# Conditioning units spread over other phases, one bank of their sums per chunk, and a phase's first splits issued ahead of its border

## The chip, the cores and the metric

The kernel runs on one core of one Trainium2 chip. The metric is the device time of one execution in microseconds (us). The kernel before takes 1564.28 us, the median of 3 runs (1564.01 to 1564.74). In the profile TensorE is PE (PEld is its weight load), VectorE is DVE, ScalarE is ACT, GpSimd is POOL, and SyncE (SP) issues the transfers of the weights.

## The reference, cut to what matters

256 tokens of width 1024 go through two blocks, all in float32. The first block has a gating mixer and an MLP, then an attention mixer and an MLP. The second block is conditioned by a vector `c`:

```python
cond = jax.nn.silu(c)
for i in range(2):
    mod = (cond @ ada_w[i] + ada_b[i]).reshape(B, 3, 3, 1024)   # ada_w[i]: 1024 x 9216
    shift, scale, gate = mod[:, :, 0], mod[:, :, 1], mod[:, :, 2]
    h = modulate(rms_norm(x, norm_g[i, 0]), shift[:, 0], scale[:, 0])
    x = x + 0.5 * gate[:, 0] * swiglu(h, ffn_w_in[i, 0], ffn_w_out[i, 0])   # 1024 -> 2 x 2816 -> 1024
    h = modulate(rms_norm(x, norm_g[i, 1]), shift[:, 1], scale[:, 1])
    x = x + gate[:, 1] * (pool_mixer(h) if i == 0 else conv_mixer(h))
    h = modulate(rms_norm(x, norm_g[i, 2]), shift[:, 2], scale[:, 2])
    x = x + 0.5 * gate[:, 2] * swiglu(h, ffn_w_in[i, 1], ffn_w_out[i, 1])
return rms_norm(x, final_g)
```

Each layer `i` of the second block has three sublayers, so there are six: ffn0, pool, ffn1, ffn2, conv_in/conv_out, ffn3. Each needs a shift, a scale and a gate of 1024 numbers out of `cond @ ada_w`.

## The kernel before, in words

**Phases and slabs.** The program is a fixed list of phases: gate_in, positions, gate_out, mlp0, qkv, attn, attn_out, mlp1, ffn0, pool, ffn1, ffn2, conv_in, conv_out, ffn3. All weights arrive in slabs of 128 x 2048 floats (1 MB, two transfers of 512 KB each) in a ring of 5 buffers. A float32 product is made of three matmuls: the weight is split into `w_hi` (a rounded copy) and `w_lo` (the rest), and so are the activations. ACT writes `w_hi` of a slab (`split_hi`, L527) and DVE writes `w_lo` (`split_lo`, L868), as soon as ACT is done. Both are called by `ahead(g)`, which splits slab g + 3 while PE works near slab g. A slab's buffer is loaded anew once PE has used the slab five earlier.

**Chunks.** An mlp phase has 8 chunks of 4 slabs and an ffn phase has 11 chunks of 3 slabs. In a chunk PE does the up product of chunk c (48 matmuls for two token tiles, t = 0 and 1), then the down product of chunk c - 1, and then it transposes `mid`, the activated result of chunk c (L1422), into one of the two banks of `tr_ps`. In an ffn, ACT takes the silu of the up product (`pre`, L769), DVE multiplies (`mid`, L1181), and after the transpose ACT writes `hT_hi` (L537) and DVE `hT_lo` (L878). In the last chunk of an ffn PE runs: up product, transpose of tile 0, part of the down products, transpose of tile 1, and the rest of the down products in halves of 512 columns, each of which signals `acc_ready`.

**Borders.** Between two phases stands `enter`. DVE adds the two halves of tile 0 to the residual (L977 and L980), ACT squares and sums them (L547), POOL makes the inverse root in two small steps (`msq`, L499, and `rstd`, L493), DVE scales the rows (`xn`, L884), and PE transposes them (L1422). Then tile 1 follows in the same way, while PE begins the next phase with tile 0. The lists `before` and `after` of `enter` name slabs that are split inside the border: `before` between the residual of tile 0 and its scaling on DVE, and ahead of the squares on ACT, `after` behind the border.

**Conditioning.** `cond @ ada_w` isn't done on PE. Its 9216 columns per layer are 18 units of 512 columns, 36 in all. A unit is loaded in two halves of 1 MB by ACT's queue (`load_ada`, L596), and DVE multiplies each half into `ada_acc` in four steps (`ada`, L938 and L941), which leaves partial sums over 128 partitions. `load_ada` makes ACT wait until DVE has used the buffer that is loaded over. `ADA_AT` says which units a phase does. Before, mlp0 does 8, qkv 2, mlp1 8, ffn0 9 and ffn1 9, and the last half unit of an ffn is done by DVE in the first chunk of the next phase (`rest`, `carried`). For a shift and a scale, `modulation` has PE transpose 16 tiles of `ada_acc` into four banks (L1509), and DVE sums each bank (`mod_sum`, L952). Before, all of a sublayer stands in chunk 1 of a phase: sublayer 0 in mlp1, 1 and 2 in ffn0, 3 in ffn1, 4 and 5 in ffn2.

**qkv.** It has 9 chunks of 2 slabs. ACT copies the product of a chunk out of PSUM (L692), PE transposes the copies (L1422), and DVE copies the transposed ones (L1091).

## Time and profile before

| | us |
|---|---|
| median of 3 runs | 1564.28 (1564.01 to 1564.74) |
| the profiled execution: its own time | 1563.99 |
| its span, from the first to the last instruction | 1562.2 |
| PE busy | 1493.4 (96% of the span) |
| DVE busy | 1051.0 (67%) |
| ACT busy | 703.7 (45%) |
| POOL busy | 39.1 (3%) |
| mean granted PE clock | 0.984 of full speed |

PE is busy for nearly the whole span, so the table alone says little on what a change of the other engines is worth. What is to be read are the places at which PE sits idle, and the stretches in which its clock is at half. The chain of waits puts 85% of the span on PE, 7% on DVE, 3% on ACT and 1% on POOL.

### The profile page before, as it was taken

The numbers are of one execution on the slowest core, as the hardware profiler recorded it, in microseconds if no ns is written. First come the engines' busy times: TensorE is split into PE (matmuls) and PEld (weight loads), VectorE is DVE, ScalarE is ACT, GpSimd is POOL, SyncE is SP. The second block draws the span as 40 slices with busy tenths as digits, with TensorE's granted clock in tenths as the row PEclk, the third lists the DMA queues.
The fourth block names the chain that finished last, engine by engine and source line by source line (L and its number), as shares of the span: only waits on it lengthen the run. The fifth ranks groups of instructions, "written<-read, shape, count | busy, mean of one in ns | idle before, by whom it ended". The sixth has DMA issues, their size and how long they took to land.

```text
span 1562.2 us, 17186 instructions
## 1 busy us (share of the span) xinstructions
PE 1493.4 (96%) x6957; PEld 1222.2 (78%) x6957; DVE 1051.0 (67%) x1222; ACT 703.7 (45%) x882; POOL 39.1 (3%) x63
## 2 busy tenths in 40 slices
PE   6899999999899999899997999998999989999998
PEld 4788888888687888688886788886888877778886
DVE  5658767675667677678786778877545464764454
ACT  5345444544654445534433443444344354454442
POOL 1000000000000000100000000000000000000000
PEclk9999999999999999999999999999999999999999
DMA  7448778665467888479893489985566545455552
GB/s 265 161 161 324 275 261 286 229 238 179 122 214 253 291 292 290 163 248 320 301 317 118 133 299 317 321 276 175 162 188 189 188 156 194 135 171 188 188 186 89
DMA packets 202267, 346.19 MB, mean 222 GB/s; under 512 B 9627, under 2 KB 105123, under 8 KB 202188
## 3 DMA queue, kind: packets, MB, share of 16 engines
q1 hardware_dynamic: 164172, 269.58, 52.0%
q10 hardware_dynamic: 38016, 75.50, 13.4%
q8 instruction: 56, 0.92, 0.2%
q14 instruction: 23, 0.19, 0.0%
HBM read 343.96 MB, written 1.09 MB: 221 GB/s over the span
## 4 chain that ended last, share of the span: by engine, by line
PE 85%; DVE 7%; ACT 3%; POOL 1%; issue 1%; DMA 0%; SPq 0%; DVEq 0%; POOLq 0%; ACTq 0%
PE up_ps L1327 52%; PE acc L1327 28%; PE tr_ps L1422 4%; DVE w_lo L868 1%; DVE ada_acc L941 1%; ACT w_hi L527 1%; POOL msq L499 1%; DVE res L980 1%; ACT xn L547 1%; DVE xn L977 1%; PE tr_ps L1509 1%; PE tr_ps L1612 1%; POOL rstd L493 1%; DVE xn L884 0%; DMA raw<-in_a_w_in 0%
## 5 line engine op out<-in xcount | busy, mean ns | idle before, releaser
L868 DVE TENSOR_TENSOR w_lo<-raw,w_hi 128x2048 fp32r<-128x2048 f32 x245 | 555.4, 2288 | 190.5 <-ACT w_hi L527 190.3
L1327 PE MATMUL up_ps<-w_hi,xT_hi 128*128 128x512 f32 x1264 | 503.3, 398 | 8.1 <-DVE xT_lo L898 7.0
L1327 PE MATMUL up_ps<-w_hi,xT_lo 128*128 128x512 f32 x1264 | 494.9, 392 | 0.0
L1327 PE MATMUL up_ps<-w_lo,xT_hi 128*128 128x512 f32 x1264 | 494.4, 391 | 0.0
L527 ACT ACTIVATE w_hi<-raw 128x2048 fp32r<-128x2048 f32 x245 | 460.2, 1915 | 41.8 <-DVE ada_acc L941 13.0
L1327 PEld LDWEIGHTS up_ps<-w_hi,xT_hi 128*128 128x128 f32 x1264 | 239.2, 189 | 61.6 <-DVE w_lo L868 6.4
L1327 PEld LDWEIGHTS up_ps<-w_hi,xT_lo 128*128 128x128 f32 x1264 | 238.5, 189 | 51.0
L1327 PEld LDWEIGHTS up_ps<-w_lo,xT_hi 128*128 128x128 f32 x1264 | 239.2, 189 | 47.1
L1327 PE MATMUL acc<-w_hi,hT_hi 128*128 128x512 f32 x624 | 199.6, 394 | 0.0
L1327 PE MATMUL acc<-w_hi,hT_lo 128*128 128x512 f32 x624 | 198.0, 391 | 0.0
L1327 PE MATMUL acc<-w_lo,hT_hi 128*128 128x512 f32 x624 | 197.8, 391 | 0.0
L941 DVE SCALAR_TENSOR_TENSOR ada_acc<-ada_raw,cond,ada_acc 128x512 f32<-128x512 f32 x252 | 189.2, 751 | 9.3 <-DMA ada_raw<-in_ada_w 1.6
L537 ACT ACTIVATE hT_hi<-tr_ps 128x256 fp32r<-128x256 f32 (+1 forms) x120 | 47.3, 439 | 248.8 <-PE tr_ps L1422 248.6
L769 ACT ACTIVATE pre<-up_ps 128x256 f32<-128x256 f32 x88 | 33.9, 385 | 264.5 <-PE up_ps L1327 264.4
L1327 PEld LDWEIGHTS acc<-w_hi,hT_lo 128*128 128x128 f32 x624 | 117.7, 189 | 24.8
L1327 PEld LDWEIGHTS acc<-w_lo,hT_hi 128*128 128x128 f32 x624 | 117.7, 189 | 24.4
L1327 PEld LDWEIGHTS acc<-w_hi,hT_hi 128*128 128x128 f32 x624 | 116.8, 189 | 23.5 <-issue 0.2
L878 DVE TENSOR_TENSOR hT_lo<-tr_ps,hT_hi 128x256 fp32r<-128x256 f32 (+1 forms) x120 | 54.5, 491 | 86.6 <-ACT hT_hi L537 86.3
L1181 DVE TENSOR_TENSOR mid<-pre,up_ps 128x256 f32<-128x256 f32 x88 | 35.1, 417 | 80.5 <-ACT pre L769 80.5
L499 POOL TENSOR_SCALAR msq<-sumsq 128x1 f32<-128x1 f32 x24 | 19.6, 818 | 1469.0 <-ACT xn L547 1468.8
L547 ACT ACTIVATE xn<-res 128x512 f32<-128x512 f32 x48 | 30.6, 638 | 50.8 <-DVE res L980 41.5
L640 ACT ACTIVATE pre<-up_ps 128x512 f32<-128x512 f32 x32 | 19.3, 602 | 73.0 <-PE up_ps L1327 73.0
(126 smaller groups left out, 824.7 us busy)
## 6 DMA issues: line engine op xcount, KB each, us to landing
raw<-in_ffn_w_in SPq DMA_DIRECT2D x176, 512.0 KB, 4.9
ada_raw<-in_ada_w ACTq DMA_DIRECT2D x72, 1024.0 KB, 7.5
raw<-in_ffn_w_out SPq DMA_DIRECT2D x88, 512.0 KB, 4.6
raw<-in_w_up SPq DMA_DIRECT2D x64, 512.0 KB, 5.6
raw<-in_w_down SPq DMA_DIRECT2D x64, 512.0 KB, 4.5
raw<-in_b_w_qkv SPq DMA_DIRECT2D x36, 512.0 KB, 4.6
raw<-in_conv_w_in SPq DMA_DIRECT2D x24, 512.0 KB, 4.4
raw<-in_a_w_in SPq DMA_DIRECT2D x16, 512.0 KB, 7.4
```

Source lines behind the costliest of these rows:

```text
L499: nc.gpsimd.tensor_scalar(msq[:, t:t + 1], src, by, EPS, op, ALU.add).then_inc(msq_ready, 1)
L527: nc.scalar.activation(w_hi[:, slot, :], raw[:, slot, :], ACT.Copy).then_inc(hi_ready, 1)
L537: nc.scalar.activation(dst, src, ACT.Copy).then_inc(tr_hi, 1)
L547: nc.scalar.activation(xn[:, t, cols], res[:, t, cols], ACT.Square, scale=D ** -0.5, accum_out=sumsq[:, t, c:c + 1]).then_inc(sumsq_ready[ ...
L640: nc.scalar.activation(pre[:, t, :], up_ps[:, t, :], ACT.Relu).then_inc(relu_done, 1)
L769: nc.scalar.activation(pre[:, t, 0:HALF], up_ps[:, t, 0:HALF], ACT.Silu).then_inc(silu_done, 1)
L868: nc.vector.tensor_tensor(w_lo[:, slot, :], raw[:, slot, :], w_hi[:, slot, :].bitcast(F32), ALU.subtract).then_inc(lo_ready, 1)
L878: nc.vector.tensor_tensor(lo, src, hi.bitcast(F32), ALU.subtract).then_inc(tr_read, 1)
L941: a = nc.vector.scalar_tensor_tensor(out=dst, in0=src, scalar=cond[:, k:k + 1], in1=dst, op0=ALU.mult, op1=ALU.add)
L1181: nc.vector.tensor_tensor(mid[:, t, 0:HALF], pre[:, t, 0:HALF], up_ps[:, t, HALF:UPN], ALU.mult).then_inc(ffn_mid, 1)
L1327: return nc.tensor.matmul(dst, a, b, start=start, stop=stop, skip_group_check=True)
L1422: last = nc.tensor.transpose(dst[:, q * P:(q + 1) * P], tile, order)
```

## The change

It has five parts. (1) qkv does 4 units in place of 2, a half of one in each of eight chunks, and ffn0 and ffn1 do 8 in place of 9, in chunks 2 to 9, so that the last chunk (10) of an ffn has none and nothing is carried into the next phase. `ADA_ORDER` takes units 16 and 17 ahead of 10 to 15, whose columns hold attention's bias rows. (2) The 16 transposes of a modulation are spread over four chunks from chunk 2 on, one bank per chunk, behind the first two up tiles; DVE sums one bank per chunk. (3) In the last chunk of an ffn the first two slabs of the next phase are split: on ACT one ahead of the two silus and one between the two `hT_hi`; on DVE both stand before the second `hT_lo`. (4) `enter` has no `before` slab at the borders into pool, ffn2, conv_in and ffn3. (5) conv_out's end splits four slabs in place of three. The core of the diff:

```diff
-ADA_AT = {"mlp0": 0, "qkv": MLP_CHUNKS, "mlp1": MLP_CHUNKS + 2, "ffn0": ADA_UNITS, "ffn1": ADA_UNITS + FFN_CHUNKS - 2}
+ADA_ORDER = [*range(10), 16, 17, *range(10, 16), *range(ADA_UNITS, 2 * ADA_UNITS)]
+ADA_AT = {"mlp0": 0, "qkv": MLP_CHUNKS, "mlp1": MLP_CHUNKS + 4, "ffn0": ADA_UNITS + 2, "ffn1": ADA_UNITS + FFN_CHUNKS - 1}
...
-    return p.tr + NORM_FILLS + TT * c + (MOD_FILLS * len(MODS.get(name, ())) if c else 0)
+    return p.tr + NORM_FILLS + TT * c + min(max(c - 1, 0), MOD_FILLS * len(MODS.get(name, ())))
+def mod_of(name, c):
+    m, q = divmod(c - 2, MOD_FILLS)
+    return (MODS[name][m], q) if 0 <= m < len(MODS.get(name, ())) else (None, None)
...
             for c in range(6):
                 g = p.slab + 2 * c
-                for u, s in (((0, 0), (0, 1)), (), ((1, 0),), ((1, 1),), (), ())[c]:
-                    load_ada(ADA_AT["qkv"] + u, s)
+                if c == 0:
+                    load_ada(ADA_AT["qkv"], 0)
+                load_ada(ADA_AT["qkv"] + (c + 1) // 2, (c + 1) % 2)
                 ahead(g)
...
                 def step(c, g):
-                    if unit0 is not None and c >= 2:
+                    with_ada = unit0 is not None and 2 <= c < FFN_CHUNKS - 1
+                    if with_ada:
                         load_ada(unit0 + c - 2, 0)
                     ahead(g)
...
+                    if c == FFN_CHUNKS - 1:
+                        ahead(g + 1)
+                        for t in range(TT):
+                            gates(c, t, g)
+                        transposed(c, 0, 2)
+                        ahead(g + 2)
+                        transposed(c, 1, 2)
+                        return
...
-            enter("ffn2", affine(3), [last("ffn2") - 1], [last("ffn2")], 3)
+            enter("ffn2", affine(3), (), [last("ffn2")], 3)
-            enter("conv_in", affine(4), [last("conv_in") - 1], [last("conv_in")], 4)
+            enter("conv_in", affine(4), (), [last("conv_in")], 4)
...
-            for k in range(-1, 2):
+            for k in range(-1, 3):
                 ahead(g + k)
-            enter("ffn3", affine(5), [last("ffn3") - 1], [last("ffn3")], 5)
+            enter("ffn3", affine(5), (), [last("ffn3")], 5)
...
-                if 1 <= c <= 4:
-                    ada(ADA_AT["qkv"] + (c - 1) // 2, (c - 1) % 2)
+                ada(ADA_AT["qkv"] + c // 2, c % 2)
...
                 def step(c, g):
                     ahead(g)
+                    if c == FFN_CHUNKS - 1:
+                        if unit0 is None:
+                            ahead(g + 1)
+                        for t in range(TT):
+                            gated_mid(c, t)
+                        transposed(c, 0, 2)
+                        if unit0 is not None:
+                            ahead(g + 1)
+                        ahead(g + 2)
+                        transposed(c, 1, 2)
+                        return
...
+                    mod_sums(name, c)
...
-                def between(s, t):                               # PE, ffn
+                def between(c, s, t):
...
-                    elif t != s:
-                        for m in mods[:1]:
-                            modulation(name, m, s)
+                    elif (s, t) == (0, 1):
+                        modulation(name, c)
```

The changed line numbers run ahead of those before: `w_hi` is L545 after, `w_lo` L895, `hT_lo` L905, the residual L1007 and L1010, the scaling L911.

VectorE at the end of ffn1 and at the border into ffn2, before: (`ada_acc` is the conditioning, `w_lo` a split, `xn<-acc` and `res` the residual of tile 0, and `xn<-res,rstd` its scaling)

```order
L938 TENSOR_SCALAR ada_acc<-ada_raw,cond 128x512 [waits ada_landed0]
L941 SCALAR_TENSOR_TENSOR ada_acc<-ada_raw,cond,ada_acc 128x512 [waits ada_step] x3
L1181 TENSOR_TENSOR mid<-pre,up_ps 128x256 [waits silu_done] x2
L878 TENSOR_TENSOR hT_lo<-tr_ps,hT_hi 128x2x128 [waits tr_hi] x2
L868 TENSOR_TENSOR w_lo<-raw,w_hi 128x2048 [waits hi_ready]
L977 SCALAR_TENSOR_TENSOR xn<-acc,region 128x512 [waits acc_ready,gate_ready]
L980 TENSOR_TENSOR res<-res,xn 128x512 [waits dve_step]
L977 SCALAR_TENSOR_TENSOR xn<-acc,region 128x512 [waits acc_ready]
L980 TENSOR_TENSOR res<-res,xn 128x512 [waits dve_step]
L868 TENSOR_TENSOR w_lo<-raw,w_hi 128x2048 [waits hi_ready]
L884 TENSOR_SCALAR xn<-res,rstd 128x512 [waits rstd_ready0]
```

The same place on VectorE in the changed kernel:

```order
L1210 TENSOR_TENSOR mid<-pre,up_ps 128x256 [waits silu_done] x2
L905 TENSOR_TENSOR hT_lo<-tr_ps,hT_hi 128x2x128 [waits tr_hi]
L895 TENSOR_TENSOR w_lo<-raw,w_hi 128x2048 [waits hi_ready] x2
L905 TENSOR_TENSOR hT_lo<-tr_ps,hT_hi 128x2x128 [waits tr_hi]
L1007 SCALAR_TENSOR_TENSOR xn<-acc,region 128x512 [waits acc_ready,gate_ready]
L1010 TENSOR_TENSOR res<-res,xn 128x512 [waits dve_step]
L1007 SCALAR_TENSOR_TENSOR xn<-acc,region 128x512 [waits acc_ready]
L1010 TENSOR_TENSOR res<-res,xn 128x512 [waits dve_step]
L911 TENSOR_SCALAR xn<-res,rstd 128x512 [waits rstd_ready0]
```

The conditioning of the last chunk is gone, both splits stand between the two `hT_lo`, and none is left between the residual and the scaling.

ScalarE at the same border, before (`w_hi` is a split, `xn,sumsq` the squares of tile 0):

```order
L596 DMA ada_raw<-in_ada_w 128x4x512 [waits ada_step]
L769 ACTIVATE pre<-up_ps 128x256 [waits up0_ready]
L769 ACTIVATE pre<-up_ps 128x256 [waits slab_used]
L537 ACTIVATE hT_hi<-tr_ps 128x2x128 [waits tr_ready] x2
L527 ACTIVATE w_hi<-raw 128x2048 [waits raw_landed3]
L527 ACTIVATE w_hi<-raw 128x2048 [waits raw_landed4]
L547 ACTIVATE xn,sumsq<-res 128x512 [waits res_ready0] x2
```

and in the changed kernel:

```order
L545 ACTIVATE w_hi<-raw 128x2048 [waits raw_landed3]
L790 ACTIVATE pre<-up_ps 128x256 [waits up0_ready]
L790 ACTIVATE pre<-up_ps 128x256 [waits slab_used]
L555 ACTIVATE hT_hi<-tr_ps 128x2x128 [waits tr_ready]
L545 ACTIVATE w_hi<-raw 128x2048 [waits raw_landed4]
L555 ACTIVATE hT_hi<-tr_ps 128x2x128 [waits tr_ready]
L565 ACTIVATE xn,sumsq<-res 128x512 [waits res_ready0] x2
```

The split of buffer 3 moved ahead of both silus, and that of buffer 4 between the two `hT_hi`.

ScalarE in the middle of qkv (chunks 3 and 4), before:

```order
L596 DMA ada_raw<-in_ada_w 128x4x512 [waits ada_step]
L527 ACTIVATE w_hi<-raw 128x2048 [waits raw_landed3]
L692 ACTIVATE mid<-up_ps 128x512 [waits up0_ready]
L692 ACTIVATE mid<-up_ps 128x512 [waits slab_used]
L527 ACTIVATE w_hi<-raw 128x2048 [waits raw_landed4]
L527 ACTIVATE w_hi<-raw 128x2048 [waits raw_landed0]
L692 ACTIVATE pre<-up_ps 128x512 [waits up0_ready]
```

and in the changed kernel:

```order
L614 DMA ada_raw<-in_ada_w 128x4x512 [waits ada_step]
L545 ACTIVATE w_hi<-raw 128x2048 [waits raw_landed3]
L711 ACTIVATE mid<-up_ps 128x512 [waits up0_ready]
L711 ACTIVATE mid<-up_ps 128x512 [waits slab_used]
L545 ACTIVATE w_hi<-raw 128x2048 [waits raw_landed4]
L614 DMA ada_raw<-in_ada_w 128x4x512 [waits ada_step]
L545 ACTIVATE w_hi<-raw 128x2048 [waits raw_landed0]
L711 ACTIVATE pre<-up_ps 128x512 [waits up0_ready]
```

A load with its wait for VectorE now stands ahead of the first split of every chunk, where before it stood so in chunks 2 and 3 alone.

## Rows read from the trace of the kernel before

**Rows 1.** Waits of PE: who waited for whom, us in total, times, longest us.

```profile
PE tr_ps L1422 <- DVE xn L884: 18.1, 10, 4.0
...
PE tr_ps L1327 <- DVE xn L884: 5.7, 1, 5.7
...
PE tr_ps L1509 <- DVE mod_sum L952: 2.1, 2, 1.5
...
PE tr_ps L1422 <- DVE mid L1181: 1.4, 2, 0.7
PE tr_ps L1422 <- DVE mod_sum L952: 1.3, 4, 0.4
```

**Rows 2.** Timeline, DVE, border into ffn2: start, us, instruction, count, [idle before <-releaser].

```profile
1046.55 0.42 DVE L878 TENSOR_TENSOR hT_lo<-tr_ps,hT_hi 128x256 fp32r<-128x256 f32 x1 [0.62 <-ACT hT_hi L537]
...
1051.33 2.29 DVE L868 TENSOR_TENSOR w_lo<-raw,w_hi 128x2048 fp32r<-128x2048 f32 x1 [1.38 <-ACT w_hi L527]
1053.54 0.68 DVE L977 SCALAR_TENSOR_TENSOR xn<-acc,region 128x512 f32<-128x512 f32 x1
...
1056.19 2.28 DVE L868 TENSOR_TENSOR w_lo<-raw,w_hi 128x2048 fp32r<-128x2048 f32 x1
1059.32 0.88 DVE L884 TENSOR_SCALAR xn<-res,rstd 128x512 f32<-128x512 f32 x2 [0.85 <-POOL rstd L493]
```

**Rows 3.** Timeline, ACT, the same border.

```profile
1049.39 3.72 ACT L527 ACTIVATE w_hi<-raw 128x2048 fp32r<-128x2048 f32 x2
```

**Rows 4.** Timeline, POOL, borders into ffn1 and into ffn2.

```profile
860.50 0.30 POOL L499 TENSOR_SCALAR msq<-sumsq 128x1 f32<-128x1 f32 x1 [18.69 <-ACT xn L547]
...
1057.13 1.51 POOL L499 TENSOR_SCALAR msq<-sumsq 128x1 f32<-128x1 f32 x1 [188.22 <-ACT xn L547]
```

**Rows 5.** Timeline, PE: transposes of tiles 0 and 1, ffn2, conv_in, ffn3.

```profile
1059.86 1.97 PE L1422 MATMUL tr_ps<-flip,xn 128*128 128x128 f32 x8 [3.94 <-DVE xn L884]
...
1069.06 1.04 PE L1422 MATMUL tr_ps<-flip,xn 128*128 128x128 f32 x8
...
1263.16 1.47 PE L1422 MATMUL tr_ps<-flip,xn 128*128 128x128 f32 x8 [3.96 <-DVE xn L884]
...
1271.28 1.09 PE L1422 MATMUL tr_ps<-flip,xn 128*128 128x128 f32 x8
...
1363.49 1.09 PE L1422 MATMUL tr_ps<-flip,xn 128*128 128x128 f32 x8 [1.01 <-DVE xn L884]
...
1370.49 1.09 PE L1422 MATMUL tr_ps<-flip,xn 128*128 128x128 f32 x8
```

**Rows 6.** Busy us by stretch; PEclk is the granted clock, 1.00 is full.

```profile
1060.00:1065.00 5.00, 5.00 (x16) 4.27 (x17) 3.45 (x8) 3.52 (x10) 0.00 (x0) 0.50 0.00 0
1364.00:1370.00 6.00, 5.99 (x30) 4.66 (x28) 5.03 (x13) 4.24 (x12) 1.12 (x2) 1.00 0.83 275
```

**Rows 7.** Slab transfers issued at 1243.5:1244.5, 1039.5:1040.5: count, KB, median us to landing.

```profile
raw<-in_conv_w_in SPq DMA_DIRECT2D x2, 512.0 KB, 4.5
...
raw<-in_ffn_w_in SPq DMA_DIRECT2D x2, 512.0 KB, 7.9
```

**Rows 8.** The chain, one chunk's up product in qkv: start, us, what, count.

```profile
348.44 10.90 PE up_ps L1327 x48
```

**Rows 9.** The instructions on mod_sum: ns min/median/max, first and last start.

```profile
L952 DVE TENSOR_REDUCE mod_sum<-tr_ps x24: 678/682/692, 469.5 to 1102.4; 128x4 f32<-128x512 f32 x24
```

**Rows 10.** Timeline, DVE, a middle chunk of ffn0.

```profile
723.54 2.29 DVE L868 TENSOR_TENSOR w_lo<-raw,w_hi 128x2048 fp32r<-128x2048 f32 x1 [1.35 <-ACT w_hi L527]
```

**Rows 11.** Timeline, ACT and DVE, end of conv_out.

```profile
1353.19 1.92 ACT L527 ACTIVATE w_hi<-raw 128x2048 fp32r<-128x2048 f32 x1 [4.31 <-DMA raw<-in_ffn_w_in]
...
1357.15 0.69 DVE L977 SCALAR_TENSOR_TENSOR xn<-acc,region 128x512 f32<-128x512 f32 x1 [5.15 <-PE acc L1327]
```

**Rows 12.** Timeline, ACT and DVE, chunk 2 of qkv.

```profile
319.49 1.92 ACT L527 ACTIVATE w_hi<-raw 128x2048 fp32r<-128x2048 f32 x1 [5.54 <-DVE ada_acc L941]
...
323.76 1.29 DVE L1091 COPY region<-tr_ps 128x512 f32<-128x512 f32 x2
```

More of the change, by code:

```diff
@@ L68, with ada_steps @@
 N_ROWS = sum(n for _, n in ROWS.values())
-ADA_AT = {"mlp0": 0, "qkv": MLP_CHUNKS, "mlp1": MLP_CHUNKS + 2, "ffn0": ADA_UNITS, "ffn1": ADA_UNITS + FFN_CHUNKS - 2}
+ADA_ORDER = [*range(10), 16, 17, *range(10, 16), *range(ADA_UNITS, 2 * ADA_UNITS)]
+ADA_AT = {"mlp0": 0, "qkv": MLP_CHUNKS, "mlp1": MLP_CHUNKS + 4, "ffn0": ADA_UNITS + 2, "ffn1": ADA_UNITS + FFN_CHUNKS - 1}
+def ada_steps(first, last):
+    return 8 * (1 + max(ADA_ORDER.index(u) for u in range(first, last + 1)))
 MODS = {"mlp1": (0,), "ffn0": (1, 2), "ffn1": (3,), "ffn2": (4, 5)}
@@ L695, in _ @@
                 g = p.slab + 12 + 2 * b
+                if b == 0:
+                    load_ada(ADA_AT["qkv"] + 3, 1)
                 ahead(g)
@@ L795, in ffn @@
                 ahead(g + 1)
-                transposed(0)
+                for t in range(TT):
+                    transposed(0, t)
                 for c in range(1, FFN_CHUNKS):
@@ L801, in _ @@
             ffn("ffn0")
-            enter("pool", None, [last("pool") - 1])
+            enter("pool", None)
             for q in range(POOLS):
@@ L1101, in _ @@
                     ahead(g + 1)
+                    ada(ADA_AT["qkv"] + 3, b)
             def logits(i):
@@ L1216, in ffn @@
                 ahead(g + 1)
-                transposed(0)
+                for t in range(TT):
+                    transposed(0, t)
                 for m in GATES[name]:
                     gate(m)
-                if carried is not None:
-                    carried()
                 for c in range(1, FFN_CHUNKS):
                     step(c, g + 3 * c - 1)
-                def rest():
-                    if unit0 is not None:
-                        ada(unit0 + FFN_CHUNKS - 3, 1)
-                return rest
             def block_norm(t):
@@ L1234, in _ @@
             enter("ffn0", residual(last("ffn0"), 3), [last("ffn0") - 1], [last("ffn0")], block_norm)
-            rest = ffn("ffn0", 0)
-            enter("pool", residual(last("pool"), 4, 0.5, 0), [last("pool") - 1])
+            ffn("ffn0", 0)
+            enter("pool", residual(last("pool"), 4, 0.5, 0), ())
             dve.wait_ge(sums_ready, 1)
@@ L1255, in _ @@
             enter("ffn1", residual(last("ffn1"), 5, 1.0, 1), (), [last("ffn1")])
-            rest = ffn("ffn1", 2, rest)
-            enter("ffn2", residual(last("ffn2"), 6, 0.5, 2), [last("ffn2") - 1], [last("ffn2")])
-            ffn("ffn2", 3, rest)
-            enter("conv_in", residual(last("conv_in"), 7, 0.5, 3), [last("conv_in") - 1], [last("conv_in")])
+            ffn("ffn1", 2)
+            enter("ffn2", residual(last("ffn2"), 6, 0.5, 2), (), [last("ffn2")])
+            ffn("ffn2", 3)
+            enter("conv_in", residual(last("conv_in"), 7, 0.5, 3), (), [last("conv_in")])
             p = at["conv_in"]
@@ L1309, in _ @@
             conv_split(KT - 2)
-            for k in range(-1, 2):
+            for k in range(-1, 3):
                 ahead(g + k)
-            enter("ffn3", residual(last("ffn3"), 8, 1.0, 4), [last("ffn3") - 1], [last("ffn3")])
+            enter("ffn3", residual(last("ffn3"), 8, 1.0, 4), (), [last("ffn3")])
             ffn("ffn3", 5)
@@ L1499, in _, with modulation @@
             down_last(p.slab + 2, xT_hi, xT_lo, 4, False, (p.tr, 2), lambda: turn_norm("mlp0", 0))
[L1501 to L1510 removed]
+            def modulation(name, c):
+                sub, q = mod_of(name, c)
+                if sub is None:
+                    return
+                layer, s = divmod(sub, 3)
+                if q == 0:
+                    pe.wait_ge(ada_step, ada_steps(layer * ADA_UNITS + 6 * s, layer * ADA_UNITS + 6 * s + 3))
+                fill = mod_fill(at[name], name, c)
+                dst = bank(fill)
+                for f in range(FILL):
+                    n = s * 3 * KT + q * FILL + f
+                    last = nc.tensor.transpose(dst[:, f * P:(f + 1) * P], ada_acc[:, n * P:(n + 1) * P], ident)
+                last.then_inc(tr_ready, 1)
             def mlp(name, after, early=True):
```

109 lines of the change are left out of this document (42 added, 67 removed).

## The prediction, made before the changed kernel ran

> **What bounds the kernel now.** I read the page first: PE is busy for 96% of the span, as the table above has it. Nothing in the change takes work off PE. It has the same matmuls and transposes, so it can only shorten the stretches in which PE waits or runs at half clock. The second view is therefore the list of PE's waits [rows 1]. The reader is to see two kinds that the change touches: waits for the scaled rows `xn` at the borders (18.1 us in ten waits, and 5.7 at the pool border), and 4.8 us of waits for DVE inside the chunks. The third is the timeline of DVE, ACT and POOL at one border, for what starts late there [rows 2 to 4]. The fourth is the granted clock behind the border [rows 5, 6].
>
> At the border into ffn2 the chain runs as follows. ACT makes two splits from 1049.39 on, 3.72 us [rows 3]. DVE's `w_lo` of the first of them starts at 1051.33, and only behind it, at 1053.54, can DVE begin the residual of tile 0. Squares follow, POOL starts `msq` at 1057.13, DVE scales at 1059.32, and PE transposes at 1059.86 after 3.94 us idle [rows 2, 4, 5]. The borders into pool and conv_in have the same order of instructions.
>
> **The change part by part.**
>
> *Splits off the border, no unit in the last chunk (three borders).* Two things move the residual of tile 0 forward. DVE's conditioning stood ahead of `mid` in the last chunk of ffn0 and ffn1, and PE waited 1.4 us in two waits for it [rows 1]. That goes. And ACT makes the first split of the next phase before the silus. So on DVE: the first `hT_lo` at 1046.55 - 0.65 = 1045.9, 0.4 for it, two splits at 2.21 each (1051.33 to 1053.54, start to start), the second `hT_lo` 0.35, which gives 1051.05 in place of 1053.54 [rows 2]. I take 2.5 us for this border and as much for the two like it, 7.5 in all. In ffn2 there is no unit to remove, but there the first split goes ahead of `mid`, so only one is left between the two `hT_lo`, and the sum is the same within 0.1. What hides the two splits now is the down product, of 24 matmuls on tile 0 and 12 on tile 1. PE needs the second `hT_lo` only at its last 12, some 9 us behind the first transpose. The condition is that the second slab has landed. Without conditioning loads in flight a slab's transfers take 4.5 us, with them 7.9 [rows 7]. It is issued near 1039.6, so it is there by 1045 in the first case, and the last chunk now has none of them.
>
> *The split between residual and scaling (four borders).* It looks free, since DVE waits for POOL anyway. It isn't. DVE's split runs from 1056.19 to 1058.47, and POOL's `msq`, started inside it at 1057.13, takes 1.51 us and ends at 1058.64, 0.17 behind the split. With DVE idle the same instruction takes 0.30 [rows 2, 4]. So a POOL step waits for the split to end, and the chain with it. Taken away, it gives 1.21 us at pool, ffn2, conv_in and ffn3: 4.8 us. Nothing is put in its place on DVE.
>
> *The clock behind two borders.* After the waits of 3.94 and 3.96 us PE ran at 0.50, the level of 1.2 GHz; after one of 1.01 us it stayed at 1.00, 2.4 GHz [rows 5, 6]. From the transposes of tile 0 to those of tile 1 it took 9.20 us into ffn2, 8.12 into conv_in and 7.00 into ffn3. The wait that is left is 3.94 - 2.5 - 1.21 + 0.65 (PE arrives earlier) = 0.9 us into ffn2 and 3.96 - 3.7 = 0.3 into conv_in. Both are below 1.01, so I expect the clock to hold and 7.00 at both: 2.2 + 1.1 = 3.3 us. The pool border keeps 5.7 - 3.7 + 0.7 = 2.7 us of waiting. That lies between the two cases, and I take nothing for it; bounds 0 and 2.
>
> *Modulations, one bank per chunk.* Before, PE waited 2.1 us ahead of its own transposes of `ada_acc` and 1.3 us ahead of those of `mid`, both for a bank that DVE had not yet summed [rows 1]. With one bank per chunk, PE issues it behind half of the up product of 10.9 us [rows 8], when the bank has long been read, and needs the next bank some 11 us later. All 3.4 us go. DVE's sum of a bank is 0.68 us [rows 9], with two small steps some 1.1. In the middle chunks of ffn0 DVE idles 1.35 us right behind that place, waiting for ACT [rows 10], so it is covered, with 0.2 us to spare once in four chunks. If that cover were gone it would cost at most 1.1 in each of four chunks.
>
> *conv_out.* The fourth split moves ahead of the residual. ACT has it done at 1355.11, DVE would run it to 1357.34, and the residual could begin at 1357.15 [rows 11]. That is 0.2 us lost, against the 1.21 above.
>
> *qkv, four units.* The chunks, 10.9 us each, get a half unit in eight cases of nine [rows 8], 3.1 us on DVE, and a load on ACT that waits for DVE's half unit of the chunk before, ahead of the first split. Before, two of nine chunks had this wait. In chunk 2 ACT's split started at 319.49 after 5.54 idle; it took 1.92, DVE's split behind it 2.29, and the copies that PE waits for began at 323.76, just as they were due [rows 2, 12]. So this loop already had no slack there, and its cost in the trace is 0. Followed through all chunks with these durations, the split comes about 0.2 us later in chunk 2 and touches the due time in chunk 5, and elsewhere it has over 1 us. I take 0.3. The bounds are 0 and, if the wait reached PE in all eight chunks by a full half unit, 8 x 3.1 = 25 us; the row lies at the low end.
>
> *Sum.* 7.5 + 4.8 + 3.3 + 3.4 - 0.2 - 0.3 = 18.5 us off the profiled execution's 1563.99, which is 1545.5. The median of the runs was 0.3 above that execution, so 1545.8.
>
> **Rivals.**
>
> *The POOL step is slow by itself.* Its 1.51 us came after 188 us of idleness, the 0.30 after 19 [rows 4]. If it is slow after a long rest, the 4.8 us don't come, the wait into ffn2 stays at 2.1 and its clock may fall: 1545.8 + 4.8 + 2.2 = 1552.8. Against it: the slow case ends 0.17 us behind the end of a split, which a rest would not arrange. The Trainium skill, SBUF — State Buffer, section "Who interferes with whom", says that a VectorE instruction with two SBUF inputs contends with a GpSimd instruction that reads SBUF, and that the second one blocks in full; by that rule, whose two inputs here are `raw` and `w_hi`, the 1.21 us go, and the trace agrees.
>
> *The clock falls all the same* after 0.9 us, because DVE's chain leaves further short waits: 3.3 us stay, 1549.1.
>
> *The slab lands late or ACT holds up the transpose.* If the second slab takes the 7.9 us of before [rows 7], ACT's split ends near 1050.4, DVE's near 1052.7 and the residual begins near 1053.2, as before, at two borders: 5 us stay and the clock's 2.2 with them, 1553.
>
> *Slower: the loop in qkv decides.* ACT waits for DVE's half unit ahead of a split, DVE waits for that split, then does PE's copies and its own splits, and only then the next half unit. If one turn is longer than a chunk, PE waits in each of eight. Its price has to pass 18.8 us, 2.4 us a chunk, to make the kernel slower. DVE's work is 2 x 2.29 + 3.1 + at most 2.6 of copies, 10.3 of 10.9 us, so it just fits. At the full 3.1 a chunk the time is 1545.8 + 24.5 = 1570.
>
> **How the numbers follow.** All terms as forecast 0.58; the clock falls 0.12; the late slab 0.12; the slow POOL step 0.07; qkv costs some us more than forecast (1 to 5) 0.08; qkv decides 0.03. The likeliest is 1545.8. The range of 1542.8 to 1552.8 takes in the pool border's clock and a residual that starts half a microsecond earlier at one end, and the rivals up to the slow POOL step at the other. Runs of this kernel can't tell less than about 0.2% (3 us) from no change. Only the last case reaches that region, or qkv in its worse part with a rival beside it: faster 0.95, the same 0.02, slower 0.03.
>
> **What would show it right or wrong.** `msq` of tile 0 at 0.30 us and DVE idle behind the residual, at four borders. The residual of tile 0 about 6 us behind the end of the last up product. Waits for `xn` at about 0.9 into ffn2 and 0.3 into conv_in, a granted clock of 1.00 behind both, and 7.0 us between the transposes of the two tiles. No wait for `mod_sum`. In qkv, ACT idle ahead of the first split of every chunk with `ada_acc` as releaser, and PE's waits for the copies (L1091) within 0.5 us of before. I am wrong if those waits grow to microseconds, if `msq` stays at 1.5 us, or if the second `hT_hi` waits for a transfer.

## The result and the profile after

The changed kernel takes 1543.68 us, the median of 4 runs (1543.10 to 1543.98), against 1564.14 for the kernel before on the same chip (4 runs). The two medians have a ratio of 0.9869; the ratio on record is 0.9862, with a 95% interval of 0.9848 to 0.9875. By that, the 1564.28 that stood ahead of the prediction would become 1542.7. The forecast was 1545.8, and its range began at 1542.8. So the change saves 20 to 22 us and not 18.5. The profiled execution took 1543.98 with a span of 1542.2, 20.0 less than before.

The page after, busy times by engine:

```profile
PE 1488.7 (97%) x6957; PEld 1217.7 (79%) x6957; DVE 1050.0 (68%) x1222; ACT 703.9 (46%) x882; POOL 34.2 (2%) x63
```

DVE's and ACT's work is what it was. PE's busy time fell by 4.7 us with the same instructions, because more of them ran at full clock: the mean granted clock rose from 0.984 to 0.989. The waits of PE after (us in total, times, longest):

```profile
PE tr_ps L1446 <- DVE xn L911: 10.2, 8, 3.3
...
PE up_ps L1351 <- DVE xT_lo L925: 6.5, 4, 3.8
...
PE tr_ps L1351 <- DVE xn L911: 2.7, 1, 2.7
...
PE tr_ps L1446 <- DVE region L1120: 1.1, 2, 0.6
```

Beside [rows 1]: the waits for `xn` fell from 18.1 to 10.2 us, the one into pool from 5.7 to 2.7, and those for `mod_sum` and `mid` are gone from the list. The timeline of DVE and POOL at the border into ffn2, which answers to [rows 2, 4]:

```profile
1044.50 0.42 DVE L905 TENSOR_TENSOR hT_lo<-tr_ps,hT_hi 128x256 fp32r<-128x256 f32 x1
1044.84 0.68 DVE L1007 SCALAR_TENSOR_TENSOR xn<-acc,region 128x512 f32<-128x512 f32 x1
...
1049.41 0.88 DVE L911 TENSOR_SCALAR xn<-res,rstd 128x512 f32<-128x512 f32 x2 [1.84 <-POOL rstd L511]
```

```profile
1048.43 0.30 POOL L517 TENSOR_SCALAR msq<-sumsq 128x1 f32<-128x1 f32 x1 [185.83 <-ACT xn L565]
```

DVE is now idle for 1.84 us behind the residual, and `msq` takes 0.30 us after 186 us of rest. PE's transposes of tiles 0 and 1 at ffn2, then tile 0 at conv_in, beside [rows 5]:

```profile
1049.95 1.09 PE L1446 MATMUL tr_ps<-flip,xn 128*128 128x128 f32 x8 [0.95 <-DVE xn L911]
...
1056.96 1.09 PE L1446 MATMUL tr_ps<-flip,xn 128*128 128x128 f32 x8
...
1245.51 1.09 PE L1446 MATMUL tr_ps<-flip,xn 128*128 128x128 f32 x8
```

The wait into ffn2 is 0.95 us and the one into conv_in too short to be listed; from tile 0 to tile 1 it now takes 7.0 us at both. The granted clock behind the border into ffn2 is 1.00 (the last figure but two), where it was 0.50 before [rows 6]:

```profile
1050.00:1056.00 6.00, 5.99 (x30) 4.76 (x31) 5.45 (x13) 4.25 (x12) 0.73 (x2) 1.00 0.49 156
```

To see where each microsecond went I cut both traces at PE's transposes of `xn` (the rows "tr_ps<-flip,xn" and, for pool, "tr_ps<-region,xn") and compared the pieces:

| piece, from start to start of the transposes | before | after | saved |
|---|---|---|---|
| start to tile 1 of mlp0 | 109.05 | 109.68 | -0.6 |
| qkv, tile 1 to chunk 5's | 67.91 | 68.16 | -0.25 |
| mlp1, tile 1 to ffn0's tile 0 | 184.17 | 182.62 | 1.55 |
| ffn0, tile 0 to tile 1 | 10.54 | 10.08 | 0.4 |
| ffn0, tile 1 to pool | 199.79 | 195.12 | 4.7 |
| pool | 19.24 | 18.73 | 0.5 |
| ffn1, tile 1 to ffn2's tile 0 | 189.36 | 185.66 | 3.7 |
| ffn2, tile 0 to tile 1 | 9.20 | 7.01 | 2.2 |
| ffn2, tile 1 to conv_in's tile 0 | 194.10 | 188.55 | 5.55 |
| conv_in, tile 0 to tile 1 | 8.12 | 7.00 | 1.1 |
| conv_in, tile 1 to ffn3's tile 0 | 92.21 | 91.04 | 1.2 |

All other pieces agree within 0.15 us; together they are 0.1 longer after. A piece can also change by chance: from the start to tile 1 of mlp0, nine profiled executions took between 109.05 and 110.4 us, and nothing is edited there.

### The profile page after: what moved, and what is told of

Its sections match the earlier page's. It is cut to its first block, busy times and chain, and to the rows that moved or that the text cites. A ratio compares the mean times of both kernels' runs of the same rounds, so it can differ in the third digit from the quotient of the medians.

```text
span 1542.2 us, 17180 instructions
## 1 busy us (share of the span) xinstructions
PE 1488.7 (97%) x6957; PEld 1217.7 (79%) x6957; DVE 1050.0 (68%) x1222; ACT 703.9 (46%) x882; POOL 34.2 (2%) x63
## 4 chain that ended last, share of the span: by engine, by line
PE 84%; DVE 8%; ACT 4%; POOL 1%; issue 1%; DMA 1%; SPq 0%; ACTq 0%; DVEq 0%; POOLq 0%
PE up_ps L1351 52%; PE acc L1351 27%; PE tr_ps L1446 3%; DVE w_lo L895 2%; ACT w_hi L545 2%; DVE res L1010 1%; ACT xn L565 1%; DVE xn L1007 1%; POOL msq L517 1%; DVE ada_acc L968 1%; PE tr_ps L1537 1%; POOL rstd L511 1%; DVE xn L911 1%; PE tr_ps L1639 1%; DMA raw<-in_a_w_in 0%
## 5 line engine op out<-in xcount | busy, mean ns | idle before, releaser
L895 DVE TENSOR_TENSOR w_lo<-raw,w_hi 128x2048 fp32r<-128x2048 f32 x245 | 555.6, 2289 | 188.2 <-ACT w_hi L545 188.0
L545 ACT ACTIVATE w_hi<-raw 128x2048 fp32r<-128x2048 f32 x245 | 461.1, 1916 | 67.2 <-DVE ada_acc L968 37.0
L905 DVE TENSOR_TENSOR hT_lo<-tr_ps,hT_hi 128x256 fp32r<-128x256 f32 (+1 forms) x120 | 54.4, 491 | 80.0 <-ACT hT_hi L555 80.0
L1446 PEld LDWEIGHTS tr_ps<-flip,mid 128*128 128x128 f32 x320 | 39.0, 140 | 10.4 <-issue 2.1
```

The source lines that it names most:

```text
L545: nc.scalar.activation(w_hi[:, slot, :], raw[:, slot, :], ACT.Copy).then_inc(hi_ready, 1)
L895: nc.vector.tensor_tensor(w_lo[:, slot, :], raw[:, slot, :], w_hi[:, slot, :].bitcast(F32), ALU.subtract).then_inc(lo_ready, 1)
L905: nc.vector.tensor_tensor(lo, src, hi.bitcast(F32), ALU.subtract).then_inc(tr_read, 1)
L1446: last = nc.tensor.transpose(dst[:, q * P:(q + 1) * P], tile, order)
```

## The experiments

Twelve kernels ran, in three groups of four, each group on one chip with the kernel before. The ratios below are against that kernel on the same chip. On those chips the kernel before took 1565.49, 1566.92 and 1565.57 us, and its runs spread over 7 us. PE's clock falls to half for a few stretches that are not the same in each execution (more on this under the third group). So small effects are read from the pieces, as above, and the times are given beside them.

### First group: the parts, and what holds POOL

**Modulations alone** (kernel before with part 2 only):

```diff
-                    elif t != s:
-                        for m in mods[:1]:
-                            modulation(name, m, s)
+                    elif (s, t) == (0, 1):
+                        modulation(name, c)
```

> The kernel before with one part of the change alone: the transposes and sums of a modulation go one bank per chunk (chunks 2 on) in place of all in chunk 1; units, splits and borders stay as before. The forecast's step counted only the modelled idle of PE, 3.4 us: 1564.1 - 3.4 = 1560.7. The trace of the changed kernel says more: a chunk with a bank takes 17.29 us against 16.81 without one, and chunks 1 and 2 of ffn2 together took 36.52 before and 34.73 with the same work spread out, so 1.8 us in ffn2, 1.0 in ffn0, 1.5 in mlp1: 4.3, which gives 1559.8. If the step is worth neither and the missing time came from elsewhere, 1560.7 or more.

Measured: 1560.57 us, ratio 0.9968 (0.9959 to 0.9977), so 3.6 to 6.4 us less than before. By the pieces, mlp1 fell from 184.17 to 182.61, ffn0 from 199.79 to 199.15, and ffn2 from 194.10 to 192.35: 1.56 + 0.64 + 1.75 = 3.95. That is between the two expectations, and above the idle time that the list of waits shows: 1.46 us in one wait in mlp1, 0.63 in two in ffn0, 1.27 in three in ffn2, 3.36 in all. All borders kept their waits (5.68, 3.96, 3.96).

**Splits back** (changed kernel without parts 3 to 5):

```diff
-            enter("ffn2", residual(last("ffn2"), 6, 0.5, 2), (), [last("ffn2")])
+            enter("ffn2", residual(last("ffn2"), 6, 0.5, 2), [last("ffn2") - 1], [last("ffn2")])
```

and so at the other borders, in `step` and in conv_out.

> The changed kernel with parts 3 to 5 undone: the second split of the next phase again between residual and scaling at the borders into pool, ffn2, conv_in and ffn3, the last chunk splits only one slab and behind both transposed halves, conv_out's end splits three. Units and modulations stay as changed. With ACT's two splits from 1042.6 on, DVE's first runs 1044.55 to 1046.8, the residual starts near 1046.8 in place of 1044.84, 2.0 later at three borders, msq is held 1.2 at four, and the clock falls again behind ffn2 and conv_in (3.3) and stays low longer behind pool (0.5): 6.0 + 4.8 + 3.3 + 0.5 = 14.6, so 1543.7 + 14.6 = 1558.3. If the second term is nothing (msq not held by the split) 1553.5; if the clock does not follow the wait, 1554.5.

Measured: 1562.27 us, ratio 0.9969 (0.9953 to 0.9985). The runs fell into groups near 1557.4, 1562.3 and 1565.5, whose mean granted clocks on record are 0.985, 0.981 to 0.983, and 0.980; the lowest group fits the expectation, and the profiled one (1565.83) had further half-clock stretches ahead of mlp0 and in attention, where nothing was edited. The waits of tile 0, at ffn2 and at conv_in:

```profile
1063.33 1.97 PE L1441 MATMUL tr_ps<-flip,xn 128*128 128x128 f32 x8 [3.96 <-DVE xn L910]
...
1264.36 1.97 PE L1441 MATMUL tr_ps<-flip,xn 128*128 128x128 f32 x8 [3.96 <-DVE xn L910]
```

They are the waits of before, though no unit stands in the last chunk. So the units did nothing for the border itself. Their gain is the wait for `mid`. In the kernel with modulations alone two such waits are left, shown as 0.81 and 0.65 us; here they are gone, and the two pieces are 1.03 (199.15 to 198.12) and 0.91 (189.55 to 188.64) shorter. Against the changed kernel this one loses 3.0 us ahead of pool, 3.0 ahead of ffn2, 3.8 ahead of conv_in and 1.1 ahead of ffn3, and from before to after the same pieces gained, without modulations, 4.0, 3.7, 3.8 and 1.2.

**An instruction with two SBUF operands in the gap** (changed kernel):

```diff
+            def extra(name):
+
+                free = region[:, 4096:6144] if name == "pool" else ada_acc[:, 0:2048]
+                nc.vector.tensor_tensor(free, ada_acc[:, 2048:4096], ada_acc[:, 4096:6144], ALU.add)
...
+                if name in ("pool", "ffn2", "conv_in", "ffn3"):
+                    extra(name)
                 scale_tokens(NORM[name], 0)
```

> The changed kernel with one instruction added on DVE between the residual of tile 0 and its scaling at the borders into pool, ffn2, conv_in and ffn3: a sum of two SBUF operands of 128x2048 whose result nobody reads, as long as the split that stood there before. It takes some 2.3 us and ends 0.3 behind the present start of the scaling. If a POOL step waits for such an instruction, msq of tile 0 goes from 0.30 to 1.5 us and ends 0.17 behind it, the scaling comes 1.2 later at four borders, and the wait into ffn2 grows from 0.95 to 2.15 with half the clock behind it (2.2): 4.8 + 2.2 = 7.0, 1550.7, less 0.3 where a border has slack. If msq is slow for another reason (its rest), only the 0.3 at four borders: 1545.

**The same with an operand from PSUM:**

```diff
+                nc.vector.tensor_tensor(free[:, 0:D], acc[:, 0, :], ada_acc[:, 2048:2048 + D], ALU.add)
+                nc.vector.tensor_tensor(free[:, D:D + 512], acc[:, 0, 0:512], ada_acc[:, 2048:2560], ALU.add)
```

> The same place and about the same DVE time as in the kernel with two SBUF operands, but with one operand from PSUM (two instructions of 128x1024 and 128x512, some 1.9 us together). If it is the pair of SBUF operands that holds POOL, msq stays at 0.30 us and the time within 0.5 us of the changed kernel: 1543.7 to 1544.2. If any busy DVE holds it, as with the two SBUF operands: 1550.

Measured: 1549.51 us (ratio 0.9905, 0.989 to 0.992) and 1543.33 us (0.9859, 0.9845 to 0.9874). The border into ffn2 with two SBUF operands, DVE and POOL:

```profile
1049.35 2.28 DVE L930 TENSOR_TENSOR ada_acc<-ada_acc 128x2048 f32<-128x2048 f32 x1
1052.48 0.88 DVE L911 TENSOR_SCALAR xn<-res,rstd 128x512 f32<-128x512 f32 x2 [0.84 <-POOL rstd L511]
```

```profile
1050.29 1.51 POOL L517 TENSOR_SCALAR msq<-sumsq 128x1 f32<-128x1 f32 x1 [186.90 <-ACT xn L565]
```

and with one operand from PSUM:

```profile
1047.38 1.22 DVE L930 TENSOR_TENSOR ada_acc<-acc,ada_acc 128x1024 f32<-128x1024 f32 x1
1048.51 0.68 DVE L931 TENSOR_TENSOR ada_acc<-acc,ada_acc 128x512 f32<-128x512 f32 x1
1049.29 0.88 DVE L911 TENSOR_SCALAR xn<-res,rstd 128x512 f32<-128x512 f32 x2
```

```profile
1048.32 0.30 POOL L517 TENSOR_SCALAR msq<-sumsq 128x1 f32<-128x1 f32 x1 [185.99 <-ACT xn L565]
```

In the first, `msq` ends at 1051.80, 0.17 behind the end of DVE's instruction. In the second DVE is busy too when `msq` starts, with an instruction that runs until 1048.60, and `msq` takes 0.30. At the other three edited borders it is the same: 1.51 us in the first kernel, 0.30 in the second. So the forecast's step is shown, and the rival of a POOL step that is slow after a rest falls: the rest was 186 to 187 us in both. The four pieces ahead of the edited borders are 1.2 us longer in the first kernel than in the second, 4.8 in all (forecast 4.8). One point of the expectation was wrong. Behind a wait of 2.17 us into ffn2 the clock did not fall:

```profile
1053.02 1.09 PE L1453 MATMUL tr_ps<-flip,xn 128*128 128x128 f32 x8 [2.17 <-DVE xn L911]
1060.03 1.09 PE L1453 MATMUL tr_ps<-flip,xn 128*128 128x128 f32 x8
```

The rest of the 6.2 us between the two kernels came at pool (0.4) and behind the border into ffn1 (0.9), where the half-clock stretches lay otherwise.

### Second group: the clock, and the loop in qkv

**Filler on PE, kernel before:** transposes of the identity into the bank that comes next.

```diff
+            def warm(n, tr):
+                pe.wait_ge(tr_read, tr - 1)
+                for _ in range(n):
+                    nc.tensor.transpose(tr_ps[:, tr % 2, 0:P], ident, ident)
```

> The kernel before, with 28 transposes of the identity on PE (about 3.05 us at full clock, into a bank of tr_ps that the next fill overwrites) ahead of its wait for xn at the borders into ffn2 and conv_in, so that PE is busy for all but 0.9 us of the wait of 3.95. If it is PE's idleness that brings the half clock behind these borders, the granted clock stays at 1.00 and the way from the transposes of tile 0 to those of tile 1 falls from 9.20 and 8.12 us to 7.0: 3.3 us less, 1564.1 - 3.3 = 1560.8. If the half clock came from elsewhere (the same work of the other engines, a fixed place in time), it stays and the time with it.

Measured: 1565.76 us, ratio 0.9988 (0.9975 to 1.0), so 0 to 4 us less; the time alone doesn't tell. The trace does. PE at ffn2, then at conv_in:

```profile
1062.95 3.22 PE L1437 MATMUL tr_ps<-flip 128*128 128x128 f32 x28
1067.07 1.09 PE L1423 MATMUL tr_ps<-flip,xn 128*128 128x128 f32 x8 [0.90 <-DVE xn L885]
1074.07 1.09 PE L1423 MATMUL tr_ps<-flip,xn 128*128 128x128 f32 x8
...
1268.13 1.09 PE L1423 MATMUL tr_ps<-flip,xn 128*128 128x128 f32 x8 [0.90 <-DVE xn L885]
1275.14 1.09 PE L1423 MATMUL tr_ps<-flip,xn 128*128 128x128 f32 x8
```

From tile 0 to tile 1 it takes 7.00 and 7.01 us in place of 9.20 and 8.12 [rows 5]: 3.3 us, as the forecast's term has it. Nothing was edited on the other engines, so it is PE's idleness that lowers its clock at these two borders.

**Filler on PE, changed kernel**, at the four waits that a half-clock stretch still follows.

> The changed kernel with the same kind of filler ahead of the four waits of PE that a half-clock stretch still follows: 22 transposes ahead of the transposes in gate_out (wait 3.33), 12 at the border into ffn0 (2.19), 16 into pool (2.69), 23 into ffn1 (3.33). If the idle time decides, the half clock goes at all four: 2.2 us at ffn1, about 2 at ffn0, 1 at pool and 2 at gate_out, 7.2 in all, 1543.7 - 7.2 = 1536.5. At ffn0 a second wait of 1.40 us (for xT_lo) follows and may bring it all the same: then 1538.5. This would beat both kernels.

Measured: 1543.08 us, ratio 0.984 (0.9822 to 0.9859). The expectation was wrong in size: by the pieces gate_out gave 1.7 us and pool 0.9, but ffn1 only 0.4 (8.58 to 8.14) and ffn0 nothing. That is 3.0 us of the 7.2 forecast, and the median, against 1543.68, shows only 0.6 of it; the profiled execution (1545.27) is above it and had a half-clock stretch at 48 us. PE at the border into ffn0:

```profile
634.65 1.09 PE L1447 MATMUL tr_ps<-flip,xn 128*128 128x128 f32 x8 [0.88 <-DVE xn L912]
637.14 0.47 PE L1352 MATMUL up_ps<-w_hi,xT_hi 128*128 128x512 f32 x1 [1.40 <-DVE xT_lo L926]
642.89 0.47 PE L1352 MATMUL up_ps<-w_hi,xT_hi 128*128 128x512 f32 x1 [2.77 <-DVE xT_lo L926]
644.71 1.09 PE L1447 MATMUL tr_ps<-flip,xn 128*128 128x128 f32 x8 [0.19 <-DVE xn L912]
```

At full clock PE only comes earlier to `xT_lo`, and waits 2.77 us for it. The way from tile 0 to tile 1 is 10.06 us, as with half a clock. DVE and ACT bound this border, not PE. At ffn1 the filler did not keep the clock up all the way. The transposes of tile 0 (at 857.61) ran at full clock behind a wait of 0.81 us, but from about 859.8 on, in a second wait of 1.40 us, it was half:

```profile
857.70:859.70 2.00, 1.01 (x8) 0.77 (x8) 1.93 (x5) 1.33 (x4) 0.00 (x0) 1.00 0.38 156
860.00:863.00 3.00, 2.89 (x7) 2.37 (x8) 2.86 (x8) 2.60 (x8) 0.16 (x1) 0.50 0.00 0
```

With the same filler the last two kernels below took 7.00 (no half clock there) and 8.23 us for this way, so what it gave at ffn1 differed between executions, from 0.35 to 1.6 us.

**qkv with thin sums** (the changed kernel; of the eight steps of each of the four units seven cover 8 columns only, so most of their sums are left out):

```diff
+                    if k and ADA_AT["qkv"] <= u < ADA_AT["mlp1"]:
+                        dst, src = dst[:, 0:8], src[:, 0:8]
```

> The changed kernel, in which the four conditioning units of qkv are summed over 8 columns instead of 512 in seven of their eight steps (this leaves out most of the sums of units 8, 9, 16 and 17), while their loads and ACT's waits stay. DVE's half unit in a qkv chunk falls from 3.1 us to 0.5 or less. By the forecast the units cost PE 0.3 us, and all waits of PE for the copies in qkv are 1.1 us, so it gives between 0.3 and 1.1: 1542.6 to 1543.4. If the loop of ACT and DVE had cost microseconds that the waits do not show, 1540 or less.

**qkv with one more step per half unit**, six in all:

```diff
+                if ADA_AT["qkv"] <= u < ADA_AT["mlp1"] - 1:
+                    nc.vector.scalar_tensor_tensor(out=ada_acc[:, c0:c0 + UPN], in0=ada_raw[:, s, 0:UPN],
+                                                   scalar=cond[:, 0:1], in1=ada_raw[:, s, UPN:2 * UPN],
+                                                   op0=ALU.mult, op1=ALU.add)
```

> The changed kernel with one more DVE instruction of 128x512 (0.78 us, its result overwritten) ahead of each half of the first three of qkv's four units, six in all. By the forecast's reckoning DVE has 10.3 us of work in the fullest of the 10.9 us chunks, 0.6 to spare, so the fullest chunks run over by 0.2 and the others not: up to 1 us, 1543.7 to 1544.7. If the whole loop (ACT waits for DVE, DVE for ACT) is the limit and not DVE's work, each instruction reaches PE: 6 x 0.78 = 4.7, 1548.4.

Measured: 1543.49 us (ratio 0.985, 0.9832 to 0.9869) and 1548.84 us (0.9884, 0.9865 to 0.9903). With thin sums qkv's piece is 67.91 us, as before and 0.25 less than after, so the units cost 0.25 us there. With the further step it is 70.77, 2.6 more than after, and PE waits for the copies in two chunks:

```profile
PE tr_ps L1451 <- DVE region L1125: 3.8, 2, 1.9
```

That is neither expectation: more than the 0.2 by DVE's work alone, and half of 4.7. The rest of the 5 us in the time lies outside qkv, in half-clock stretches (404.1, 428.0 and a longer one at 858.1). The profiled execution with thin sums (1546.11) had stretches at the same places, and against it the further step costs 2.9 us, all of them in qkv. What follows is that the four units fit with less room than the forecast had reckoned.

### Third group: what a wait costs, and a faster version

**The changed kernel again:**

> The changed kernel once more, unedited, as the baseline on this chip for the other three. 0.986 of the kernel before, 1543.7 if this chip is like the first one.

Measured: 1542.93 us (1542.47 to 1544.44), ratio 0.9851 (0.9829 to 0.9873). The baseline for this group.

**27 small stops of PE in ffn3:**

```diff
+                    for n in range(PINGS):                       # POOL
+                        pool.wait_ge(slab_used, g + 3 + n)
+                        nc.gpsimd.memset(ping[:, :], 0.0).then_inc(pong, 1)
...
+                if 0 <= n < PINGS:                               # PE, behind a slab
+                    pe.wait_ge(pong, n + 1)
```

> The changed kernel with 27 small stops of PE in ffn3, behind each slab of chunks 1 to 9: POOL waits for the slab's last matmul, clears one column, and PE waits for that. It measures what a wait of PE costs beside what the profile shows as idle. In the trace of before a wait shown as 0.649 us stood between two starts that are 1.037 apart, where matmuls start 0.227 apart: 0.81 lost, 0.16 more than shown, since a matmul's record is 0.389 long and the next could start 0.227 behind it. If that holds for each wait, the way from the transposes of tile 1 of ffn3 to the end grows by the sum of the shown idle plus 27 x 0.16 = 4.4 us; if a wait costs what it shows, by the sum alone. The shown idle should be 0.4 to 0.9 each; where POOL's instruction falls beside a split on DVE it may be up to 2.3, if a write alone is held as well.

Measured: 1557.45 us, ratio 0.9952 (0.9937 to 0.9968). PE around one of the stops:

```profile
1365.23 0.39 PE L1359 MATMUL up_ps<-w_lo,xT_hi 128*128 128x512 f32 x1
1365.46 0.39 PE L1359 MATMUL up_ps<-w_hi,xT_lo 128*128 128x512 f32 x1
1366.06 0.50 PE L1359 MATMUL up_ps<-w_hi,xT_hi 128*128 128x512 f32 x1 [0.22 <-POOL ping L540]
1366.40 0.39 PE L1359 MATMUL up_ps<-w_lo,xT_hi 128*128 128x512 f32 x1
```

The idle time shown is 0.22 us at all 27, 5.8 in all; I had expected 0.4 to 0.9. The median is 14.5 above the changed kernel beside it. Matmuls start 0.23 apart, but here 0.60 and then 0.34, so a stop costs 0.37 + 0.11 = 0.48. The whole confirms it: from the transposes of tile 1 to the end it takes 204.70 us, against 191.68, which is 13.0 for 27 stops, 0.48 each. The profile shows less than half of what such a stop costs. It is short by 0.16 because a matmul's record of 0.39 us runs past the moment at which the next could have started, and by another 0.1 because the first matmul behind the stop holds up the second.

**The half-clock stretches** differ between executions. Behind one and the same wait of 3.96 us at the border into ffn2, the changed kernel with the splits back took 1.97 us for the eight transposes and 8.72 to tile 1, while the kernel with modulations alone took 1.45 and 8.10; at conv_in it was 8.93 and 8.74, against 8.12 before. In some executions a stretch of half clock lies at 48 us, in others not. Here is the same window of the kernel with splits back and of the kernel before (the granted clock is the last figure but two):

```profile
48.00:54.00 6.00, 6.00 (x16) 3.81 (x15) 4.14 (x4) 0.58 (x1) 0.00 (x0) 0.50 0.12 48
```

```profile
48.00:54.00 6.00, 6.00 (x28) 4.95 (x27) 5.93 (x8) 0.00 (x0) 1.17 (x1) 1.00 0.00 0
```

Without it the way from the start to tile 1 of mlp0 is 109.1 to 110.4 us, with it 113.7 to 114.2 in the profiled executions that took 1567.7 (filler, kernel before) and 1565.8 (splits back). That is the size of the steps between the groups of runs. Of the runs without a profile only the mean granted clock is on record. It is lower in the longer groups, as said above, but not where the stretches lie, so for them it is the likely cause and no more. A term for the clock behind one wait is uncertain by about 1 us from one execution to the next.

**Attention's split moved** (with fillers in gate_out, pool and ffn1):

```diff
-                if i == ITEMS - 4:
-                    ahead(at["attn"].slab - 1)
...
             out_hi(PAIRS - 1)
+            ahead(at["attn"].slab - 1)
```

> The changed kernel with the fillers kept at three of the four places (22 transposes in gate_out, 16 into pool, 23 into ffn1) and one more edit: the split that ACT makes in the middle of the last attention pair (1.90 us at 419.00, behind which PE waits 2.54) and DVE's half of it go behind the last copies of attention. By the way between the turns of tiles in the earlier filler run, gate_out gives 1.7, pool 0.9 and ffn1 0.4 us; the attention wait gives 2.5 and, if the half clock behind it goes too, 1 more: 5.5 to 6.5 less than the changed kernel, 1537.7. If ACT was the bound of attention all along, the other waits there grow and only its 1.9 us come.

Measured: 1537.44 us (1537.03 to 1538.55), ratio 0.9816 (0.9794 to 0.9837), 5.5 less than the changed kernel beside it. It is the fastest version. Attention's piece fell by 3.4 us (81.17 to 77.79), gate_out's by 1.7, pool's by 0.9. In the profiled execution ffn1's way from tile 0 to tile 1 fell by 1.6 as well (8.58 to 7.00), and ffn0's grew by 0.4 (10.07 to 10.51), which the edit does not touch. The wait for ACT in attention, 2.9 us in two before, is:

```profile
PE tr_ps L1647 <- ACT ada_raw L754: 1.4, 3, 0.7
```

**The border into ffn0 treated like the others**, on top of that:

```diff
+                    if name == "mlp1" and c == MLP_CHUNKS - 1:
+                        for t in range(TT):
+                            tiles = (slice(None), slice(None), slice(t * P, (t + 1) * P))
+                            lo_part(hT_hi[tiles], hT_lo[tiles], mid_fill(p, name, c) + t, h0 + 2 * c + t)
+                            ahead(g + 3 + t)
...
-            enter("ffn0", residual(last("ffn0"), 3), [last("ffn0") - 1], [last("ffn0")], block_norm)
+            enter("ffn0", residual(last("ffn0"), 3), (), [last("ffn0")], block_norm)
```

> The kernel with fillers and the moved attention split, and the border into ffn0 treated as the others were: the two splits of mlp1's last chunk stand one behind each transposed half, and none between residual and scaling. ACT's second split waits for a transfer that lands at 619.8, so DVE's ends near 624.0 and the residual starts 0.65 later than 623.34, but msq is no longer held (1.21): 0.55 less than the kernel without this edit, 1537.2. If PE's next waits there (1.40 for xT_lo) take it back, no difference.

Measured: 1538.02 us, ratio 0.9817 (0.9795 to 0.9839), no difference. The wait for `xn` fell from 2.19 to 1.58, as expected, but the next one gave it back:

```profile
627.04 1.09 PE L1457 MATMUL tr_ps<-flip,xn 128*128 128x128 f32 x8 [1.58 <-DVE xn L916]
629.53 0.47 PE L1362 MATMUL up_ps<-w_hi,xT_hi 128*128 128x512 f32 x1 [1.40 <-DVE xT_lo L930]
635.28 0.77 PE L1362 MATMUL up_ps<-w_hi,xT_hi 128*128 128x512 f32 x1 [2.74 <-DVE xT_lo L930]
```

The tiles are 10.94 us apart there, against 10.51 without this edit. So the expectation's last clause held.

## Why the prediction's sum came out short

| term | forecast | from the traces |
|---|---|---|
| splits and units at four borders (7.5 + 4.8 - 0.2) | 12.1 | 12.7 |
| modulations | 3.4 | 4.0 |
| clock behind ffn2 and conv_in | 3.3 | 3.3 |
| qkv | -0.3 | -0.25 |
| clock at pool | 0 | 0.5 |
| ffn0, tile 0 to tile 1 | not in it | 0.4 |
| start of the program | not in it | -0.6 |
| all other pieces | not in it | -0.1 |
| sum | 18.5 | 19.9 |

*Splits off the border.* Right in the mechanism, 0.6 low in size. The residual started 6.0 us behind the last up product and the wait into ffn2 fell to 0.95 us (forecast 0.9), the one into conv_in to 0.15 (forecast 0.3). How the parts share it is now known: the units give the waits for `mid`, the splits all the rest. By border it gave 4.0 (pool), 3.7, 3.8 and 1.2 us, where 3.7, 3.7, 3.7 and 1.0 stood in the sum.

*msq held by the split.* Right, and shown from both sides: put back with two SBUF operands it costs 1.2 us at each border, with one operand from PSUM nothing. The Trainium skill's rule (SBUF — State Buffer, section "Who interferes with whom") that one such VectorE instruction blocks a GpSimd instruction that reads SBUF fits: `msq` ended 0.17 us behind the VectorE instruction.

*The clock.* Right at the two borders, 3.3 us. That the fall comes from PE's idleness was an inference, and the filler showed it.

*Modulations.* This is the step that failed, in its size. "All 3.4 us go" summed what the list of waits shows as idle. The waits went, but 4.0 us came back (3.95 in the kernel with this part alone), and not 3.4. So the step took the idle time in the list for the cost of the wait, and a wait costs PE more than that. The stops in ffn3 show it directly, at 0.22 shown and 0.48 paid. The extra isn't one fixed amount: 0.26 us for each of those stops, and 0.1 for each of the six waits for `mod_sum`; why these two differ isn't shown. The two waits for `mid`, counted inside the borders at 1.4 us, were short in the same way, by about 0.2 each by the kernel with splits back. That would be most of the 0.6 by which the borders' term was low; for this the cause is in part argued.

*Pool's clock.* Taken as 0 with bounds of 0 and 2; 0.5 came. *The way into ffn0* was left out because nothing was edited there; the waits came earlier by 1.5 us against the stretches of half clock, and 0.4 us went. The kernel before with filler elsewhere has the same code there and took 10.06 us, and the changed kernel with attention's split moved took 10.51, so it lies in where the stretch fell in one execution, and not in the change. Nor was it all a gain: at 10.06 the kernel before waited 1.06 us for `mid` at the end of ffn0 in place of 0.71, and its piece up to pool took 200.14 in place of 199.79.

*The start.* The 0.6 us lost there lie within the scatter of the executions.

*Base.* The forecast added 0.3 us for the median against the profiled execution; after, the median was 0.3 below it. That is 0.6 of the 2.1 us between 1545.8 and 1543.68, and the other 1.5 is the difference of the sums.

The rivals: none came. The POOL step isn't slow by itself, the clock held, the second slab came in time (its transfers took 4.0 and 5.0 us and were there at 1038.99, ahead of ACT's split at 1039.56), and qkv did not decide. The last was closer than its chance said: one more step of 0.78 us in six half units would have cost 2.6 us there.

What stays open: what decides whether a wait lowers the clock. Behind a wait of 2.19 us into ffn0 the transposes ran at half clock in the kernel before and in the one with attention's split moved:

```profile
626.81 1.96 PE L1445 MATMUL tr_ps<-flip,xn 128*128 128x128 f32 x8 [2.19 <-DVE xn L910]
627.00:633.00 6.00, 5.01 (x16) 3.97 (x16) 1.53 (x5) 4.12 (x12) 0.69 (x2) 0.50 0.96 391
```

In the changed kernel, behind the same 2.19 us, they ran at full clock, and half of it came at about 633.2:

```profile
631.78 1.09 PE L1446 MATMUL tr_ps<-flip,xn 128*128 128x128 f32 x8 [2.19 <-DVE xn L911]
634.00:639.00 5.00, 4.72 (x11) 3.79 (x12) 1.99 (x5) 3.07 (x10) 0.86 (x2) 0.50 0.88 356
```

Behind 2.17 us into ffn2 no half clock came at all.
